# Matmuls of ones into unread banks, at the points where TensorE waits in a two-block transformer kernel

## The reference

```
mix = mixer(rms_norm(h, pre_mix_norm), ...)        # gated convolutions, 16 meta tokens in front
h = h + rms_norm(mix, post_mix_norm)               # post-norm 0
ff = swiglu(rms_norm(h, pre_ffn_norm), ...)        # D_FF = 2816
h = h + rms_norm(ff, post_ffn_norm)                # post-norm 1
# second block, two layers
x = x + even_mixer(rmsnorm(x))    # 8 stick-breaking heads and 8 sliding-window heads
x = x + swiglu_2(rmsnorm(x))
x = x + mla_mixer(rmsnorm(x))     # latent attention: c_q (384), c_kv (256), k_rope; 16 heads
x = x + swiglu_2(rmsnorm(x))
return rmsnorm(x)

# stick-breaking, per head
z = q @ k.T * scale
log_1m_beta = where(causal, log_sigmoid(-z), 0)
between = reverse_cumsum(log_1m_beta) - log_1m_beta
w = where(causal, exp(log_sigmoid(z) + between), 0)
out = w @ v
```

## Time and profile before

| | before |
|---|---|
| median of 3 runs | 1036.9 us (1036.25, 1036.9, 1043.39) |
| profiled execution, its own time | 1039.4 us |
| span of the profiled execution | 1037.6 us |
| TensorE busy | 949.3 us (91%), 7615 matmuls |
| VectorE busy | 678.7 us (65%) |
| ScalarE busy | 512.6 us (49%) |
| mean granted TensorE clock | 0.96 |
| HBM read | 146.39 MB, 142 GB/s over the span |

### The profile page before, as it was taken

The page is one execution under the profiler, slowest core; times in us unless marked ns, Lnnn a source line. Parts: engine busy times, 40 slices in busy tenths (PEclk is TensorE's granted clock), DMA queues, the critical chain, the costliest instruction groups (busy, mean ns, idle before and its releaser), DMA issues. The chain is left out here.

```text
span 1037.6 us, 20336 instructions
## 1 busy us (share of the span) xinstructions
PE 949.3 (91%) x7615; PEld 925.7 (89%) x7615; DVE 678.7 (65%) x1323; ACT 512.6 (49%) x952; POOL 59.6 (6%) x53
## 2 busy tenths in 40 slices
PE   6798887999999979857999999999879999999997
PEld 5698887999999979755999999999768899999997
DVE  4399755666756557567656766556898657667552
ACT  4643254445444436566635544445376635445443
POOL 0017500000000010000000000000100000000000
PEclk9899988999999989879999999999889999999999
DMA  7243341676666637400457665665330346765661
GB/s 207 79 125 87 117 114 51 176 210 184 183 186 182 193 92 214 140 1 1 132 144 202 191 194 168 181 191 153 108 118 2 84 144 196 205 176 168 185 190 53
DMA packets 275319, 148.56 MB, mean 143 GB/s; under 512 B 5961, under 2 KB 273210, under 8 KB 275258
## 3 DMA queue, kind: packets, MB, share of 16 engines
q1 hardware_dynamic: 274330, 146.02, 48.7%
q0 software_dynamic: 608, 1.52, 0.5%
q10 hardware_dynamic: 320, 0.20, 0.1%
HBM read 146.39 MB, written 1.06 MB: 142 GB/s over the span
## 5 line engine op out<-in xcount | busy, mean ns | idle before, releaser
L461 PE MATMUL bank<-x0h,whi 128*128 128x256 f32 (+1 forms) x1080 | 311.4, 288 | 20.3 <-DVE wlo L1448 10.6
L462 PE MATMUL bank<-x0l,whi 128*128 128x256 f32 (+1 forms) x1080 | 309.1, 286 | 0.0
L463 PE MATMUL bank<-x0h,wlo 128*128 128x256 f32 (+1 forms) x1080 | 308.8, 286 | 0.0
L1448 DVE TENSOR_TENSOR wlo<-raw,whi 128x1024 fp32r<-128x1024 f32 (+3 forms) x184 | 204.4, 1122 | 99.1 <-ACT whi L1062 98.8
L461 PEld LDWEIGHTS bank<-x0h,whi 128*128 128x128 f32 x1080 | 208.6, 193 | 24.5 <-issue 15.7
L1062 ACT CAST whi<-raw 128x1024 fp32r<-128x1024 f32 (+3 forms) x184 | 174.6, 961 | 81.2 <-PE bank L463 78.2
L463 PEld LDWEIGHTS bank<-x0h,wlo 128*128 128x128 f32 x1080 | 208.7, 193 | 0.0
L462 PEld LDWEIGHTS bank<-x0l,whi 128*128 128x128 f32 x1080 | 207.6, 192 | 0.0
L1584 DVE TENSOR_TENSOR wlo<-raw,whi 128x1024 fp32r<-128x1024 f32 x108 | 132.0, 1222 | 65.3 <-ACT whi L1144 64.5
L461 PE MATMUL bank<-x1h,whi 128*128 128x256 f32 x532 | 156.8, 295 | 17.2 <-DVE un L2051 4.5
L463 PE MATMUL bank<-x1h,wlo 128*128 128x256 f32 x532 | 154.4, 290 | 0.0
(11 more groups left out here) (247 smaller groups left out, 1283.0 us busy)
## 6 DMA issues: line engine op xcount, KB each, us to landing
raw<-in_ffn_w_gate SPq DMA_DIRECT2D x44, 512.0 KB, 4.2
raw<-in_ffn_w_up SPq DMA_DIRECT2D x44, 512.0 KB, 4.6
raw<-in_ffn_w_down SPq DMA_DIRECT2D x32, 448.0 KB, 4.2
raw<-in_w_gate SPq DMA_DIRECT2D x22, 512.0 KB, 3.9
raw<-in_w_up SPq DMA_DIRECT2D x22, 512.0 KB, 4.1
raw<-in_w_in SPq DMA_DIRECT2D x20, 512.0 KB, 3.9
raw<-in_even_w_in SPq DMA_DIRECT2D x18, 512.0 KB, 4.1
raw<-in_ffn_w_down SPq DMA_DIRECT2D x16, 512.0 KB, 4.5
```

The lines of the kernel that those rows point to most:

```text
L461: pe.matmul(o, w[0], x[0], start=first, stop=False, skip_group_check=True)
L462: pe.matmul(o, w[0], x[1], start=False, stop=False, skip_group_check=True)
L463: return pe.matmul(o, w[1], x[0], start=False, stop=last, skip_group_check=True)
L1448: ins = v.tensor_tensor(l_, x, h_.bitcast(F32), ALU.subtract)
```

## The change

Ten places in TensorE's stream get `spin(n, o)`: n matmuls of `oner` by `oner` (repeated to 256 columns) that accumulate into `o`, a part of a bank that nothing reads before a later start flag clears it. Each is a weight load and a matmul of 128x256. Post-norm 0 gets 12, 13 and 16 of them, post-norm 1 gets 9, 13 and 16, all into bank 5. In stick-breaking each `sb_sums` and each `weighted` gets 5, ahead of the wait for its operand, which is moved behind them; `weighted` spins for the stick-breaking heads alone (n < NH). The query tiles get 10 ahead of their waits and the latent attention 12. The wait for `mats_done` ahead of the first spin is one that stood later before and was over long ago there. In all 79 + 80 + 22 = 181 matmuls. No other engine's stream changes.

```diff
+            spin_x = oner[:, :].unsqueeze(1).broadcast_to([P, NB, P])
+
+            def spin(n, o):
+
+                for _ in range(n):
+                    pe.matmul(o, oner[:, :], spin_x, start=False, stop=False, skip_group_check=True)
+
@@
             for s in range(4, 8):
                 out_part(s)
+            pe.wait_ge(g("mats_done"), 2)
+            spin(12, bank[5][:, 0:T])
             stat_sum(0)
+            spin(13, bank[5][:, 0:T])
             stat_rows(0)
+            spin(16, bank[5][:, 0:T])
             gate_up(0, (x0h, x0l), x_ready(0), (g("sq_done"), SQ0["y0"] + 8), 1)
             down_stage(0)
+            spin(9, bank[5][:, 0:T])
             stat_sum(2)
+            spin(13, bank[5][:, 0:T])
             stat_rows(2)
+            spin(16, bank[5][:, 0:T])
@@ def sb_sums(h):
-                pe.wait_ge(g("sp_lo"), h + 1)
                 if h >= 2:
                     pe.wait_ge(g("sb_d"), h - 1)
                 c = bank[(6, 0)[h % 2]]
+                spin(5, c[:, 0:T])
+                pe.wait_ge(g("sp_lo"), h + 1)
@@ def weighted(n, h, pt, vsl, ready, count, done):
-                pe.wait_ge(ready, count)
                 o = bank[(7, 1)[(n // 2) % 2]]
                 if h % 2 == 0 and n >= 4:
                     pe.wait_ge(g("o_lo"), n // 2 - 1)
+                if n < NH:
+                    spin(5, o[:, T:2 * T])
+                pe.wait_ge(ready, count)
@@
             s0, t0 = SLOT0["uq"], TILE0["uq"]
+            spin(10, bank[5][:, 0:T])
             pe.wait_ge(g("cl_done"), 5)
             pe.wait_ge(g("kr_in"), 1)
@@
+            spin(12, bank[5][:, 0:T])
             pe.wait_ge(g("qn_lo"), KT)
             pe.wait_ge(g("rp_lo"), 5)
             pe.wait_ge(g("pt_lo"), NH)
```

## The result

Twenty runs of each: 1034.66 us median after (1032.84 to 1036.66), 1042.53 us median before (1036.25 to 1044.73). The ratio of the means is 0.9936, 95% interval 0.9923 to 0.9949, so the change saves 5 to 8 us. The absolute time was forecast 1033.5. So the time came out within 1.2 us of the forecast while the gain, 6.7 us by the means, was twice what was forecast. The change also narrows the spread, from 8.5 to 3.8 us.

The account below looks back on a forecast made before the run. TensorE, 91% busy, was taken as the bound, with six stretches at half clock. From 1036.9, terms -1.7, -2.2, +1.2, -0.65 and -0.8 gave 1032.75; forecast 1033.5, leaning to the smaller gain, range 1030 to 1038.5 us.

Parts of the forecast that it names:

- a spin costs 0.12 us: All spin places: one idle matmul with its weight load priced 0.12 us at full clock, 0.21 us at half.
- they fit in the waits: Both post-norms: each spin group fits in TensorE's existing wait, 0.3 to 0.7 us left, so it costs nothing.
- The rival that ones don't hold the clock: Whole kernel: products of ones don't keep the clock up, every gain is lost, 1043.2 us; chance 0.06.
- 1.7 and 2.2 us in the post-norms: First matmul to third block's sums after post-norm 0 and post-norm 1: gains of 1.7 and 2.2 us at full clock.
- +1.2 us: Stick-breaking: net loss of 1.2 us, spins on the path costing 2.4 us less 1.2 us from the faster clock.
- the walk: Stick-breaking: tracing three engines' orders gives spin delays of 0.85, 0.60, 0.60 and 0.35 us for four head pairs.
- 2.4 us walked for the spins: Stick-breaking: cost of spins on the path over four head pairs, mainly those before the odd head's weighted product.
- 1.2 for the clock: Stick-breaking: two sums steps on the path, 1.69 us cold against 1.00 warm, give back 1.2 us.
- the two latent terms: Query-side latent projections gain 1.3 us and latent attention 1.6 us, from work at full instead of half clock.
- 0.65 + 0.8: Query-side projections and latent attention: gains of 1.3 and 1.6 us at half, as the clock's fall isn't certain every run.
- The displaced scores of the latent attention: Latent attention: 12 spins push first scores 1.44 us, covered by the 1.86 us wait for VectorE's value split.
- Gained and given back: Rival: the four gains vanish behind other engines, leaving stick-breaking's cost, 1038.1 us; chance 0.20 in full or half.

## Why the prediction was right, and where it wasn't

**Right: a spin costs 0.12 us, the spins hold the clock in the post-norms, and they fit in the waits.** The rows of after have 0.12 us, 1.00 and waits of 0.20 to 0.51 us left, and A and B are 11.72 or 11.73 us in every profile with the full number there (seven for post-norm 0, six for post-norm 1); without spins none is below 13.39. The rival that ones don't hold the clock is out. It drew on the peak-current limiter, of which the Trainium skill (TensorE: Matmul & The Clock Gate, "Seeing it yourself", not the section that the prediction names) says that all-ones operands don't trip it. Whatever holds for that limiter, the clock seen here stays up on ones.

**Right: 1.7 and 2.2 us in the post-norms, against the profile at hand.** From the first matmul to the third block's sums 1.73 and 2.21 us came back, and 0.23 us more because the broadcast rows of post-norm 0 ran warm. **Mis-sized: the same terms over many executions.** I took the length of the cold stretch from one profile. Over six profiles without spins at the place, A is 13.4 to 14.9 us (mean 13.7) and B 13.9 to 18.7 (mean 15.2), against 11.72: on average 2.0 and 3.5 us, and up to 6.9. That is 1.6 us more than I counted, and perhaps still too little: three of the six profiles (those with stick-breaking, latent and post-norm 1 spins alone) are of the fastest execution of their kernel. The three runs shown misled too: I had set the sum against their median of 1036.9 and took the profiled execution for a slow one, while 1039.4 is faster than 15 of the 20.

**Stick-breaking: the mechanism right, the size uncertain.** I forecast +1.2 us, with the weighted spins on the path. Against the profile at hand S grew by 2.33 us, against the mean of ten profiles without spins (33.5) by 0.8, and the comparison of times gives 0 within 2 us either way. The path itself is shown: taking the weighted spins out made S 3.0 to 3.7 us shorter than with them, and the single steps above agree with the walk where the clock was up. Both terms seem to have been too small: 2.4 us walked for the spins against these 3.0 to 3.7 (the half clock of after's last steps included), and 1.2 for the clock against 1.4 (32.27 - 30.89) by the profile at hand or 2.6 by the mean. The 1.2 was also summed wrongly, as two steps of 0.69 are 1.38. What I missed is that without spins this stage itself lies in two heaps (32.2 to 32.4 and 34.0 to 34.5), of which I had seen the shorter.

**Not shown to be the spins': the two latent terms.** I counted 1.3 and 1.6 us for the clock in Q and M. Between the two profiles they are there: 4.77 to 3.30 and 3.69 to 2.10. But the kernel with the post-norm spins alone, which has none in these places, has 3.30 and 2.11 as well:

```profile
728.32 0.35 PE L461 MATMUL bank<-x1h,whi 128*128 128x256 f32 x1 [1.52 <-DVE x1l L1998]
731.62 0.60 PE L538 MATMUL bank<-rows,oner 128*128 128x128 f32 x4
```

```profile
728.30:731.60 3.30, 3.28 (x27) 3.30 (x28) 2.36 (x8) 0.00 (x0) 2.19 (x1) 1.00 0.58 190
```

The wait of 1.52 us before the first tile is the same as in the earlier trace rows, and the clock didn't fall. Of nine profiles without latent spins four have the long Q and two the long M; of five with them none. If the spins are what keeps the five short, they are worth 4/9 x 1.5 + 2/9 x 1.6 = 1.0 us on average (an estimate). The measured ratio (0.9986, up to 1.0004) neither shows nor excludes that, and four in nine against none in five can be chance. Halving these terms was right, and 0.65 + 0.8 was perhaps a little too much. The displaced scores of the latent attention cost nothing, as forecast: the start of the second pair waits 0.38 us for VectorE's split, not 1.86.

```profile
769.91 0.39 PE L468 MATMUL bank<-arh 64*128 64x256 f32 x2 [0.38 <-DVE vl L1874]
772.96 0.55 PE L852 MATMUL bank<-con,un 128*128 128x128 f32 x3 [1.35 <-DVE un L1980]
```

**The sum.** By the means over profiles, -2.0 - 3.5 + 0.8 - 1.0 = -5.7 us; the measured ratio gives -6.7, with 5 to 8 as its interval. Since the profiles behind the means are in part of fast executions, a sum short of the measured gain is no surprise. "Gained and given back" is out: up to the first stick-breaking sums, gate/up and the stages behind it move along with the post-norms to within 0.02 us.

**Luck in the agreement.** The forecast of 1033.5 is 1.2 us from the measured 1034.66 because two errors cancel: the base of 1036.9 was 4.4 us below the mean of before (1041.3), and the gain of 3.4 us was 3.3 short of the measured 6.7. The two profiles agree by luck as well. Their spans differ by 5.8 us and I had summed 5.6, but 1.00 of the 5.8 arose ahead of the first spin, where the change does nothing (the sums of post-norm 0 start at 159.67, not 160.67), and it makes up for most of the 1.1 us that S exceeded its term.

## What to carry to other kernels

Idle time of TensorE that is set by others can be filled with idle matmuls so that the work behind it starts at full clock; fill each wait nearly but not wholly (half as many were no better here and, it seems, less reliable), and put none between two pieces of work that follow each other, unless you have traced who waits for the second. A stretch at half clock varies from execution to execution, in whether it comes and in how long it lasts, so take several profiles of the same kernel before pricing it, and don't credit a difference of two profiles to the edit until a kernel without that edit has been seen in the same place. The median of three runs says little where the times lie in two heaps.

## What the runs showed of the hardware

The same kernel on the same inputs took 1036 to 1045 us. After post-norm 1 the clock came back 4.9 us after the first matmul in one execution and 15.3 us in another, though TensorE never paused in either. Through both post-norms products of ones with an operand read twice, one each 0.12 us, kept the clock at 1.00, where it was at 0.50 behind the waits without them. Half as many left it at 0.50 from 162.0 us on in post-norm 0 of one execution, and it was back as the first matmul began at 165.33.
